# Opening a parallel-head decoder layer: token operand E added by transfers, and two sums of weights too

## The reference, cut to what matters

```python
h = rms_norm(x, g_pre)                       # (512, 2048)
proj = h @ w_in                              # queries, keys, values and gates of three groups, and
                                             # 6 columns fb for the forget gates
log_f = log_sigmoid(fb + b_forget)           # forgetting attention of group B adds its running sum
mkv = rms_norm(mem, g_mem) @ w_mem_kv        # 256 memory tokens, keys and values of group C
y = concat(out_a * silu(ga), out_b * silu(gb), out_m * silu(gm))
x = x + rms_norm(y @ w_out, g_post)
```

## Time and profile before

| | us |
|---|---|
| median of 3 runs | 880.01 |
| the profiled execution, whole | 880.82 |
| its span, first to last instruction | 879.0 |
| PE busy | 863.6 (98%) |
| VectorE (DVE) busy | 725.3 (83%) |
| ScalarE (ACT) busy | 536.5 (61%) |
| GpSimd (POOL) busy | 77.6 (9%) |

### The profile page before, as it was taken

The page is one execution under the profiler, slowest core; times in us unless marked ns, Lnnn a source line. Parts: engine busy times, 40 slices in busy tenths (PEclk is TensorE's granted clock), DMA queues, the critical chain, the costliest instruction groups (busy, mean ns, idle before and its releaser), DMA issues.

```text
span 879.0 us, 13757 instructions
## 1 busy us (share of the span) xinstructions
PE 863.6 (98%) x5181; PEld 766.7 (87%) x5181; DVE 725.3 (83%) x1025; ACT 536.5 (61%) x918; POOL 77.6 (9%) x84
## 2 busy tenths in 40 slices
PE   9998999999999999999999999999999999999996
PEld 6997999988888888888888888888888888888885
DVE  5789789988888888888888988888888887985568
ACT  6795565665656565656565656565656586665452
POOL 0000210000000000000030304030301000000000
PEclk9999899999999999999999999999999999999998
DMA  9981577566668668667677667667654299566855
GB/s 291 304 204 25 168 172 177 129 165 168 156 178 185 152 177 181 156 179 180 156 180 180 156 180 180 156 180 180 156 132 108 98 367 320 168 216 201 287 206 191
DMA packets 179143, 161.37 MB, mean 184 GB/s; under 512 B 7353, under 2 KB 144217, under 8 KB 177670
## 3 DMA queue, kind: packets, MB, share of 16 engines
q1 hardware_dynamic: 170166, 142.66, 53.1%
q0 software_dynamic: 8704, 16.78, 14.0%
q10 hardware_dynamic: 208, 1.07, 0.3%
HBM read 152.33 MB, written 43.28 MB: 223 GB/s over the span
## 4 chain that ended last, share of the span: by engine, by line
PE 79%; DVE 13%; ACT 5%; issue 3%; DVEq 0%; POOL 0%; ACTq 0%; POOLq 0%
PE d_ps L711 19%; PE d_ps L716 10%; PE e_ps L711 10%; PE e_ps L716 5%; PE c_ps L711 5%; DVE ring L1485 3%; PE pt_ps L821 3%; PE c_ps L716 2%; PE d_ps L660 2%; PE d_ps L662 2%; PE d_ps L661 2%; DVE sums L1512 2%; PE score_ps L660 2%; PE score_ps L661 2%; PE score_ps L662 2%
## 5 line engine op out<-in xcount | busy, mean ns | idle before, releaser
L1485 DVE TENSOR_TENSOR ring<-raw,ring 128x1024 fp32r<-128x1024 f32 x134 | 164.6, 1230 | 56.9 <-ACT ring L1034 56.7
L1485 DVE TENSOR_TENSOR ring<-sums,ring 128x1024 fp32r<-128x1024 f32 x112 | 137.2, 1225 | 42.1 <-ACT ring L1034 42.1
L1034 ACT ACTIVATE ring<-raw 128x1024 fp32r<-128x1024 f32 x134 | 140.1, 1055 | 37.1 <-PE d_ps L662 12.4
L711 PE MATMUL d_ps<-late,ring 128*128 128x512 f32 x576 | 145.2, 394 | 0.0
L1034 ACT ACTIVATE ring<-sums 128x1024 fp32r<-128x1024 f32 x112 | 118.3, 1056 | 18.6 <-DVE sums L1512 15.1
L711 PEld LDWEIGHTS d_ps<-late,ring 128*128 128x128 f32 x576 | 103.4, 189 | 18.7 <-DVE five L1617 0.2
L716 PEld LDWEIGHTS d_ps<-late,ring 128*128 128x128 f32 x576 | 78.6, 190 | 5.6
L716 PE MATMUL d_ps<-late,ring 128*128 128x256 f32 x576 | 80.3, 282 | 0.0
L1512 DVE TENSOR_TENSOR sums<-raw 128x1024 f32<-128x1024 f32 x56 | 68.5, 1223 | 0.1
L1512 DVE TENSOR_TENSOR sums<-sums,raw 128x1024 f32<-128x1024 f32 x56 | 68.5, 1222 | 0.0
L2062 POOL DMA_DIRECT2D sum_dram<-in_w_out_dram x32 | 28.8, 901 | 418.2 <-DMA sum_dram<-in_w_out_dram 275.4
(11 more groups left out here) (387 smaller groups left out, 1918.0 us busy)
## 6 DMA issues: line engine op xcount, KB each, us to landing
raw<-in_w_in_dram SPq DMA_DIRECT2D x112, 512.0 KB, 6.0
sum_dram<-in_w_out_dram POOLq DMA_DIRECT2D x32, 512.0 KB, 7.4
raw<-sum_dram SPq DMA_DIRECT2D x32, 512.0 KB, 3.9
raw<-in_w_out_dram SPq DMA_DIRECT2D x24, 512.0 KB, 7.3
raw<-in_w_mem_kv_dram SPq DMA_DIRECT2D x16, 512.0 KB, 7.8
sum_dram<-in_w_out_dram SPq DMA_DIRECT2D x16, 512.0 KB, 6.6
sum_dram<-sum_dram SPq DMA_DIRECT2D x16, 512.0 KB, 6.0
stage<-in_x_dram SPq DMA_DIRECT2D x4, 1024.0 KB, 10.9
```

Source lines behind the costliest of these rows:

```text
L711: pe.matmul(bank[:], w[:, 0, k], both[:, k], start=i in (TOK_A, TOK_B) and k == 0, stop=False, skip_group_check=True)
L1034: act.activation(dst, src, ACTF.Copy).then_inc(hi_done, 1)
L1485: return dve.tensor_tensor(dst, a_, hi_.bitcast(F32), ALU.subtract)
```

## The change

It does eight things.

1. The quarter e is taken from PSUM with a negated gain (`gains_neg`, 128 x 16, made by one VectorE instruction). So B is now b + (-e), an addition, and E is held as -e + f, that is, negated; its high part is made with scale -1 and its low part as -E minus the high part.
2. That addition of f to E is no longer VectorE's: Pool issues eight transfers of 128 KB inside SBUF, each adding one k-slice of f to E (`accum_op`), with two semaphores, so two at a time. They are issued once B is made and the last tokens are taken. ACT's high part of E and VectorE's low part of F wait for all eight.
3. The first sum of weights (B of pair 0) is one transfer of 512 KB issued by Pool that adds R22 into R21 where it lies; E's sum of pair 0 is another, into a second copy of R21 that SP loads once all tokens are turned. VectorE makes neither; sums are counted by `sum_count`.
4. g - C is made right after C (`difference_g`), before the weights of A, and no longer after the sum for C.
5. The low part of F is moved from before the weights of A to behind the low part of E in the loop (after B's turn), together with the sum for F's weights.
6. The forget matmuls with F run behind product E instead of ahead of product A, and `f_low` and `f_z` come at F's turn instead of E's.
7. Tiles 4 and 5 are scaled one by one (`scale_tile`), tile 4 earlier, with a root of its own on ACT.
8. SP's loads into the slots of R11 and R21 of pair 0 wait for the low part of E's weights instead of a sum.

The core of the diff (renamed counters, semaphore declarations and the first lines of unchanged functions are left out):

```diff
@@ sync: load @@
                     if j == R22:
                         sp.wait_ge(lo_done, operand(p, TOK_G) + 1)
+                    elif j == R12:
+                        sp.wait_ge(sum_done, sum_count(p, 3))
+                    elif p > 0:
+                        sp.wait_ge(sum_done, sum_count(p, 2))
                     else:
-                        sp.wait_ge(sum_done, 4 * p + (4 if j == R12 else 3))
+                        sp.wait_ge(lo_done, operand(p, TOK_E) + 1)
@@ sync: the pairs @@
                 load_two(2)
+                if p == 0:
+                    sp.wait_ge(bank_turned, 4 * TILES)
+                    col, half = pieces[R21]
+                    sp.dma_start(sum_tile(0, 2).rearrange("p (k n) -> p k n", n=P),
+                                 w_in_v[:, KH * half:KH * (half + 1), col:col + P]).then_inc(first_e_loaded, 16)
@@ tensor @@
             forget_gates(1, TOK_D, slice(0, T2))
-            pe.wait_ge(whole_ready, 3)
-            forget_gates(3, TOK_F, slice(T2, S))
             turn_v_mem(NM - 1)
...
                     if p == 0 and i == TOK_D:
                         pe.wait_ge(late_ready, LATE_ORDER.index(TOK_E) + 1)
-                        forget_gates(2, TOK_E, slice(T2, S), final=True).then_inc(f_done, 1)
+                        forget_gates(2, TOK_E, slice(T2, S))
+                    if p == 0 and i == TOK_E:
+                        pe.wait_ge(whole_ready, 3)
+                        forget_gates(3, TOK_F, slice(T2, S), final=True).then_inc(f_done, 1)
@@ scalar @@
                 if i in SUM_OF:
-                    act.wait_ge(sum_done, 4 * p + SUM_OF[i] + 1)
+                    if p == 0 and i in (TOK_B, TOK_E):
+                        act.wait_ge(first_b if i == TOK_B else first_e, 16)
+                    else:
+                        act.wait_ge(sum_done, sum_count(p, SUM_OF[i]))
...
-                if i in (TOK_C, TOK_E):
-                    act.wait_ge(parts_made, 5)
+                if i == TOK_C:
+                    act.wait_ge(parts_made, 3)
+                if i == TOK_E:
+                    for added in e_added:
+                        act.wait_ge(added, 16 * KH // len(e_added))
...
-                if p == 0 and i == TOK_E:
+                if p == 0 and i == TOK_F:
                     act.wait_ge(f_done, 1)
@@ vector @@
-            parts_c_e(0)
+            parts_c(0)
             copy_v_mem(NM + 2)
-            parts_c_e(1)
-            lo_whole(TOK_F)
+            parts_c(1)
+            difference_g()
             lo_v_mem(1)
             copy_v_mem(NM + 3)
             lo_operand(0, 0)
-            add_weights(0, 1)
             lo_v_mem(2)
             lo_late(TOK_B)
             lo_operand(0, 1)
             lo_v_mem(3)
             add_weights(0, 2)
-            dve.wait_ge(parts_made, 5)
-            dve.tensor_tensor(token_f32(TOK_G), token_f32(TOK_G), token_f32(TOK_C), ALU.subtract).then_inc(late_f32, 1)
             lo_operand(0, 2)
             lo_late(TOK_C)
...
+                if p == 0 and i == TOK_F:
+                    dve.wait_ge(f_low, 1)
+                    dve.scalar_tensor_tensor(out=fbuf[:, 0], in0=f_ps[0:NB, :], scalar=bfor[:, 0:1], in1=fbuf[:, 1],
+                                             op0=ALU.add, op1=ALU.add).then_inc(f_z, 1)
                 if i in (TOK_D, TOK_F):
                     first_strip(p, i)
...
                 if p == 0 and i == TOK_B:
                     lo_late(TOK_E)
+                    add_weights(0, TOK_F)
+                    lo_whole(TOK_F)
@@ gpsimd @@
             pool.memset(wf[:].bitcast(F32), 0.0).then_inc(wf_cleared, 1)
+
+            piece_landed(pool, 0, R21)
+            piece_landed(pool, 0, R22)
+            pool.dma_start(sum_tile(0, 0), raw_tile(piece(0, R22)), accum_op=ALU.add).then_inc(first_b, 16)
+            pool.wait_ge(first_e_loaded, 16)
+            pool.dma_start(sum_tile(0, 2), raw_tile(piece(0, R11)), accum_op=ALU.add).then_inc(first_e, 16)
+            pool.wait_ge(parts_made, 1)
+            pool.wait_ge(bank_f32, TURNS)
+            for k in range(KH):
+                if k >= len(e_added):
+                    pool.wait_ge(e_added[k % len(e_added)], 16 * (k // len(e_added)))
+                pool.dma_start(token_f32(TOK_E)[:, k], token_f32(TOK_F)[:, k], accum_op=ALU.add
+                               ).then_inc(e_added[k % len(e_added)], 16)
             z, e, s2, p = fbuf[:, 0], fbuf[:, 1], fbuf[:, 2], fbuf[:, 3]
             pool.wait_ge(f_z, 1)
```

More of the change, by code:

```diff
@@ L85 @@
 TURNS = 4 * (TILES - MB)
-ROOTS = 4
+ROOTS = 5
 WARM_UP = 12
@@ L346, in build @@
         sum_done = sem("sum_done")
+        first_b = sem("first_b")
+        first_e_loaded = sem("first_e_loaded")
+        first_e = sem("first_e")
+        e_added = [sem(f"e_added{n}") for n in range(2)]
         used = sem("used")
@@ L1098, in take_tokens @@
                         kt = 2 * b + j
+                        gain = gains_neg[:, kt:kt + 1] if (pair, half) == (2, 0) else gains[:, 1, kt:kt + 1]
                         last = act.activation(dst[:, kt % KH], turn_ps(pair, b)[:, T2 * j:T2 * (j + 1)], ACTF.Copy,
-                                              scale=gains[:, 1, kt:kt + 1])
+                                              scale=gain)
                     last.then_inc(bank_f32, 1)
@@ L1267, in _ @@
             squares(4)
+            root(4, 4)
             hi_mem(8)
@@ L1274, in _ @@
             squares(5)
-            root(5, 4, 2)
+            root(5, 5)
             hi_mem(11)
@@ L1495, in add_weights @@
                 s = SUM_OF[i]
+                if p == 0 and i in (TOK_B, TOK_E):
+                    return
                 for j in {0: (R21, R22), 1: (R11,), 2: (R11, R21), 3: (R12,)}[s]:
@@ L1539, in rstd, with scale_tile @@
                 chain(dve.tensor_tensor(stat[:, 4, c], stat[:, 2, c], stat[:, 3, c], ALU.mult))
-            def scale_tiles(root_count, t, n=1):
-                dve.wait_ge(squares_done, t + n - 1)
-                rstd(root_count, t, n=n)
-                for i in range(t, t + n):
-                    one = stage[:, i % 4]
-                    dve.tensor_scalar(one, one, stat[:, 4, i:i + 1], None, ALU.mult).then_inc(tile_scaled, 1)
+            def scale_tile(t):
+                dve.wait_ge(squares_done, t)
+                rstd(t, t)
+                one = stage[:, t % 4]
+                dve.tensor_scalar(one, one, stat[:, 4, t:t + 1], None, ALU.mult).then_inc(tile_scaled, 1)
             def lo_memory(b0, b1):
@@ L1576, in difference_b, with parts_c @@
                 dve.wait_ge(whole_ready, 1)
-                dve.tensor_tensor(token_f32(TOK_B), token_f32(TOK_B), token_f32(TOK_E), ALU.subtract
-                                  ).then_inc(parts_made, 1)
-            def parts_c_e(half):
+                dve.tensor_tensor(token_f32(TOK_B), token_f32(TOK_B), token_f32(TOK_E), ALU.add).then_inc(parts_made, 1)
+            def parts_c(half):
                 dve.wait_ge(bank_f32, TURNS - 2 + 2 * half)
@@ L1584, in parts_c_e, with difference_g @@
                 k = slice(SUBS * half, SUBS * (half + 1))
-                f, b, c, e = (token_f32(i)[:, k] for i in (TOK_F, TOK_B, TOK_C, TOK_E))
+                f, b, c = (token_f32(i)[:, k] for i in (TOK_F, TOK_B, TOK_C))
                 dve.tensor_tensor(c, f, b, ALU.add).then_inc(parts_made, 1)
-                dve.tensor_tensor(e, e, f, ALU.subtract).then_inc(parts_made, 1)
+            def difference_g():
+                dve.wait_ge(parts_made, 3)
+                dve.wait_ge(whole_ready, 2)
+                dve.tensor_tensor(token_f32(TOK_G), token_f32(TOK_G), token_f32(TOK_C), ALU.subtract).then_inc(late_f32, 1)
             def lo_late(i):
                 dve.wait_ge(late_hi, LATE_ORDER.index(i) + 1)
-                minus(late[:, LATE[i], :, 1], token_f32(i), late[:, LATE[i], :, 0]).then_inc(late_ready, 1)
+                if i == TOK_B:
+                    dve.wait_ge(parts_made, 3)
+                if i == TOK_C:
+                    dve.wait_ge(late_f32, 1)
+                low, whole, high = late[:, LATE[i], :, 1], token_f32(i), late[:, LATE[i], :, 0]
+                if i == TOK_E:
+                    last = dve.scalar_tensor_tensor(out=low, in0=whole, scalar=-1.0, in1=high.bitcast(F32),
+                                                    op0=ALU.mult, op1=ALU.subtract)
+                else:
+                    last = minus(low, whole, high)
+                last.then_inc(late_ready, 1)
             def gated(head):
@@ L1756, in _ @@
             take_keys(3)
+            scale_tile(4)
             lo_mem(10)
@@ L1844, in after_operand @@
                     lo_late(TOK_E)
+                    add_weights(0, TOK_F)
+                    lo_whole(TOK_F)
                 if p == 0 and i == TOK_C:
                     lo_late(TOK_G)
-                if p == 0 and i == TOK_E:
-                    dve.wait_ge(f_low, 1)
```

(2 more changed lines are left out.)

38 lines of the change are left out of this document (26 added, 12 removed).

## The result

The changed kernel takes 883.46 us (median of 6 runs, 883.30 to 884.52) against 879.87 us for the kernel before (6 runs, 879.13 to 880.55): a ratio of 1.0042, 95% interval 1.0032 to 1.0052. It is **slower by 3.6 us**, where 2.4 us faster had been forecast. The profiled execution has 883.42 us, with a span of 881.6 against 879.0.

A forecast was written before the change was run, and what follows sets the result against it. PE, busy 98% of the span, was taken as the bound: 6.9 us to win in the opening, less waits of 1.9 and 2.6, left 2.4, so 880.0 - 2.4 = 877.6 us. Low 875.4, high 884.0.

The forecast's parts named there:

- Part 1: Opening up to C: 5.6 us of VectorE work leaves, C starts at 81.9, its wait falls from 3.7 to 1.9 us.
- Part 2: Transfers on Pool's queue: E lands late enough that PE waits a new 2.6 us before E's forget matmuls.
- all landed at 83.5: Last of the eight additions to E on Pool's queue; bounds 78.5 to 89.
- 3.1 us a round: Cost of two 128 KB additions to E, a quarter of the movement (1.0) plus 2.0 to 2.2 us; bounds 2.0 and 4.4.
- E lands late: Rival: E lands at 86.8, PE waits 5.9 us, low clock adds 2.6; 883.4 us; chance 0.20.
- 3 x 2.9: Products' term in the sum for the start of pair 1, forecast at 102.8 against 105.35 before.
- E lands in time: Rival: E is there by 81, PE loses only 1.9 us; 875.6 us; chance 0.17.
- I take the full clock: Behind the 1.9 us wait at C no low clock follows; the low clock had cost 2.7 us before.
- new wait of 2.6 us at E: PE may start E's forget matmuls at 90.3, where it could at 87.7.
- Part 3: Forget gate chain after the opening: gate at 108.7, 1.4 us earlier than before; 2.4 us of gain left.
- low value: Pool's time for the forget gate from f_z: 1.5 + 0.1 + 1.8 = 3.5 us, against 5.85 before.
- gate chain takes the gain: Rival: Pool again needs 5.85 us from f_z, gate at 111.0; 879.5 us; chance 0.21 with the low clock.

The follow-up runs named there:

- run 5: Changed kernel without the 512 KB transfer for E's weight sum and SP's second load of R21; VectorE makes that sum: 877.42 us, 0.9970.
- run 11: run 5's kernel with low parts of C and E ahead of their weights on VectorE and f_z at E's turn: 874.94 us, 0.9944.
- run 4: Changed kernel with four of the eight token additions issued ahead of the sum for E's weights, four behind: 880.83 us, 1.0011.
- run 3: Changed kernel with four semaphores for the additions to E, so four in flight instead of two: 879.80 us, 1.000.
- run 8: Changed kernel, transfers kept, with the low part of E ahead of the low part of E's weights on VectorE: 881.88 us, 1.0021.
- Run 2: Changed kernel with f added to E by two VectorE instructions behind the low part of C, not by transfers: 880.16 us, 1.0004.
- run 6: Run 2's kernel with the low part of token operand C ahead of C's weights on VectorE: 879.00 us, 0.9991.
- run 7: run 6's kernel with the low part of E also ahead of E's weights on VectorE: 877.71 us, 0.9975.
- run 1: Changed kernel without the eight additions of f to E, so its results are wrong: 875.49 us, 0.9950.
- run 9: run 7's kernel with f_low and f_z back at E's turn: 876.69 us, 0.9962.
- run 10: run 9's kernel with both weight sums on VectorE too, so no transfers of the change left: 877.90 us, 0.9976.

## Why the prediction was wrong

**Part 1 held.** C was forecast at 81.9 behind 1.9 us, and is at 81.44 behind 2.04; the small waits went. The clock stayed full behind it in the profile, as taken, though not for the reason given (below).

**Part 2: the mechanism was right and its size wrong.** The step that failed is "all landed at 83.5": it was 86.65. The 3.15 us are made up of four. The second load of R21, priced by its neighbour in the earlier trace rows at 5.7 us, took 8.2 (issued 0.5 us earlier than summed), so the add for E's weights was issued at 68.97 instead of 66.8: +2.15. That sum and the first addition behind it took 6.15 instead of 6.9: -0.75. The rounds behind them took 11.65 us instead of 10.3, because one of them took 4.6 us instead of 3.1: +1.35. And my own sum had a slip: 73.6 + 3 x 3.1 + 1.0 is 83.9, not 83.5: +0.4. The term of 3.1 us a round itself was good: where the sum is not in the queue, runs 5 and 11 show 3.0 behind the first round. What I had not priced is what a 512 KB transfer does to those behind it beyond its own 4 us of movement. Why the next pair still took 4.2 us, with the sum landed and the engines idle for part of it, is open; runs 5 and 11 show only that it goes with the sum. Why the load took 8.2 us wasn't tried by itself. It ran beside the transfer for B's weights, which took 8.2 us too, and only 5.5 and 5.6 in runs 5 and 11, where the load is left out: each seems to have lengthened the other. The additions issued at 64 to 65 in runs 4 and 5 took 5.6 to 6.6 us against 2.7 later, in a stretch in which the 16 DMA engines were busy throughout (share 1.12 and 0.95 from 65 to 70 us in these two runs; 0.41 from 80 to 82 in the changed kernel, where an addition took 2.7 to 3.0).

From landing to PE 6.7 us passed, for 6.8 forecast. So the rival *E lands late* is what happened, almost in its own numbers: landing 86.65 (86.8), wait 5.95 us (5.9), 883.46 us (883.4). Its clock price was too high, 1.5 us for 2.6, and pair 1 was at 107.34 for 108.7; the agreement of the total is luck to that extent: the 2.0 us at pair 1 became 3.6 because the pairs behind lost another 0.6 and because the profiled execution of before, against which the 2.0 is read, was itself 0.95 us above its median.

One more slip, without effect: in the sum at the start of pair 1 the term "3 x 2.9" must be 2 x 2.9, since only F and G follow; with it the sum is the 102.8 that stands there, and nothing is rounding. And the rival that a landing near 78 to 79 would have brought is *E lands in time*, the first of the list and not the second.

**The clock was the second step that failed,** and hidden by the first. "The longest of these waits is half of the one behind which the clock fell, so I take the full clock" was said of the wait at C, and even there it does not hold: behind 2.03 to 2.06 us at C the clock fell in runs 3, 5 and 8. For the new wait of 2.6 us at E the sum took the full clock with no reason given. Run 2 had nearly that wait (2.35) and its forget matmuls took 3.45 us for 1.9; it came to 880.16, no change, where the forecast was 2.4 us less. In run 6 the clock stayed full behind the same 2.35 us, so the price was a chance that the sum had put at nothing, not a certainty.

**Part 3 held.** Pool took 1.94 + 1.28 us for 3.5 forecast, the gate chain did not bind in the changed kernel, and the low value came much as said: right behind f_z VectorE ran only one with a PSUM operand, and Pool was well into its own when the next began. The rival *gate chain takes the gain* is real in runs 3, 6, 7 and 8: 1.4 to 2.3 us more in the column "rest" than in run 1. It isn't the fast opening that brings it: runs 1 and 5 start pair 1 at 100.09 and 101.36 and lose nothing, run 8 starts it at 103.98 and loses 2.3. It is VectorE, which there reaches f_z only behind the start of pair 1 and then goes on without a gap beside Pool's first instruction.

**The choice itself.** I had put the turning point to "slower" at a landing of 84.7, only 1.2 us behind a sum that rested on four unmeasured terms with bounds from 78.5 to 89, and yet gave that side 0.20. The bounds said more than the likeliest value did.

## What to carry to other kernels

A chain of transfers is priced from what is queued ahead of it on the same queue: ask what the first one waits for and how much it moves, before asking what each one costs; here the chain's own rounds, where nothing else was in the way, were within 0.1 us of the estimate, and the transfer ahead of them with the load that it waited for cost the gain. Within an engine's queue, put what the bound engine needs first ahead of what it needs later: two such swaps were worth 1.2 and 2.4 us of PE's waits. And after freeing a wait, look at the next chain into the same place, as its slack is what the gain is paid out of.

## What the runs showed of the hardware

**The clock behind a short wait is not settled by its length.** Behind 2.02 to 2.06 us at C, where PE had been busy before, the granted clock fell in runs 3, 5 and 8 (2.03, 2.06, 2.03) and stayed in the changed kernel and in runs 1, 2 and 4 (2.04, 2.03, 2.02, 2.05); behind 2.35 us at E it fell in run 2 and stayed in run 6. Behind the longer waits it fell each time (3.58 before, 3.95 in run 4, 5.95 in the changed kernel), behind those of 0.86 to 1.51 us never (runs 3 and 6 to 11). What decides between is open. It varies between executions of one kernel as well: of 64 executions of the kernel before in the three sets, the 35 with a mean granted clock of 0.993 took 880.5 us in the mean, the 29 with 0.995 or more 879.1. The profiled execution of before was of the first kind, so the 2.7 us that I read as the price of its low clock is likely more than its median pays. But the mean clock isn't a price by itself: in run 5, executions with 0.998 were no faster than the profiled one with 0.996.

**Transfers that add within SBUF.** 128 KB, in rows of 1 KB, took 2.7 to 3.0 us from issue to landing on quiet engines, 5.5 to 6.6 behind or beside other traffic. 512 KB took 5.3 us for E's weights and 8.2 for B's beside SP's load; without that load (runs 5 and 11) B's took 5.5 and 5.6. The DMA row of the changed kernel shows one pair at a time moving, with holes of 0.9 to 2.1 us in which nothing does.

**Pool could not issue at will.** With four semaphores (run 3) it stood 3.00 us with the sum and two additions outstanding, for nothing in the program.

**Pool beside VectorE.** Pool's first forget-gate instruction, 6x512 from SBUF to SBUF, took 1.94 us where an instruction of VectorE with two SBUF operands began some 0.7 us after it (after, runs 1, 2, 4, 5: 108.70 against 108.00 in the changed kernel), 3.16 to 3.17 where one of 1024 columns began within 0.2 us of it (3, 6, 7, 8), and 3.97 where two stood back to back behind f_z (before, 9, 10, 11). The Trainium skill (SBUF — State Buffer, Who interferes with whom) says that a VectorE instruction with two SBUF inputs contends with a GpSimd instruction that reads SBUF, and that the port pair they share is an exclusive lock. The trace agrees in kind: in all eight slow cases Pool's instruction ended 1.8 us after the end of the last VectorE instruction of those named (108.08 for 106.27 in run 3, 107.20 for 105.40 before), as if its own work, 1.5 us for its like alone, began only then. Where Pool began first, neither was held off for the whole of the other's instruction: VectorE's instruction 0.7 us behind took 1.23 us, like most, and Pool ended with it (109.94 for 109.93 in the changed kernel); one that began 0.2 us behind Pool's fourth instruction (113.05 for 112.85) took 1.48 us for 1.22, beside Pool's 1.50.
